# A hybrid decoder layer on one core: one weight split moved, exps and squares exchanged, squares summed four at a time, and a tenth buffer for expert weights

## The reference

```
u = RMSNorm(x);  proj = u @ w_in           # z, xBC, dt, q, k, v, indexer q/k/weights, two gates
A = (RMSNorm(SSD(conv(xBC), dt) * silu(z)) * ssm_norm) @ w_ssm_out   # 32 heads, width 2048
B = DSA attention (indexer picks 64 keys a query, 16 heads) @ w_att_out
x += (sigmoid(gate_ssm)*A + sigmoid(gate_att)*B) @ w_mix_out
x += CrossAttention(RMSNorm(x), RMSNorm(mem))
x += HierarchicalMoE(RMSNorm(x))           # 32 experts of 1024 -> 512 -> 1024, top 2 of 8 in one group
out = RMSNorm(x)
```

## Time and profile before

| What | us |
|---|---|
| Median of 3 runs | 1004.75 |
| Profiled execution, its time | 1004.63 |
| Its span | 1002.9 |
| PE busy | 916.0 |
| DVE busy | 448.9 |
| ACT busy | 308.4 |
| POOL busy | 107.2 |

### The profile page before, as it was taken

The page is one execution under the profiler, slowest core; times in us unless marked ns, Lnnn a source line. Parts: engine busy times, 40 slices in busy tenths (PEclk is TensorE's granted clock), DMA queues, the critical chain, the costliest instruction groups (busy, mean ns, idle before and its releaser), DMA issues.

```text
span 1002.9 us, 13810 instructions
## 1 busy us (share of the span) xinstructions
PE 916.0 (91%) x5693; PEld 634.6 (63%) x5693; DVE 448.9 (45%) x826; ACT 308.4 (31%) x503; POOL 107.2 (11%) x115
## 2 busy tenths in 40 slices
PE   3899889998999999989898999999999898898886
PEld 3799888898889999879675343434343343433432
DVE  5478997676786765365536121212121121211212
ACT  4355445667558443344323000000000000000002
POOL 1000006964662000000000000000000000000000
PEclk9899999999999999999999999999999999999999
DMA  9445354344326667755258999999999999999994
GB/s 217 151 129 179 121 160 143 111 127 127 126 86 178 200 180 283 252 168 210 84 210 323 420 421 421 422 421 421 421 422 421 422 421 422 421 421 421 421 417 172
DMA packets 111896, 278.01 MB, mean 277 GB/s; under 512 B 14866, under 2 KB 78402, under 8 KB 87770
## 3 DMA queue, kind: packets, MB, share of 16 engines
q1 hardware_dynamic: 111690, 276.61, 73.2%
q10 hardware_dynamic: 144, 0.52, 0.1%
HBM read 276.06 MB, written 1.05 MB: 276 GB/s over the span
## 4 chain that ended last, share of the span: by engine, by line
PE 58%; DMA 12%; DVE 11%; SPq 6%; issue 5%; POOL 3%; ACT 3%; DVEq 0%; POOLq 0%; ACTq 0%
PE bank L1876 14%; PE bank L1480 9%; PE bank L1481 9%; PE bank L1482 9%; DMA moe<-in_w_e_up_dram 8%; PE bank L1907 7%; SPq L385 6%; DVE lo_w L915 3%; DMA moe<-in_w_e_gate_dram 3%; POOL work L570 2%; PE bank L1843 2%; PE bank L1893 2%; ACT hi_w L596 1%; DMA moe<-in_w_e_down_dram 1%; DVE work L1072 1%
## 5 line engine op out<-in xcount | busy, mean ns | idle before, releaser
L1876 PE MATMUL bank<-moe,xg 128*64 128x512 f32 x1024 | 228.5, 595 | 19.1 <-DMA moe<-in_w_e_up_dram 9.0
L1480 PE MATMUL bank<-u_hi,hi_w 128*128 128x256 f32 x632 | 184.8, 292 | 11.3 <-DVE lo_w L915 10.4
L1482 PE MATMUL bank<-u_hi,lo_w 128*128 128x256 f32 x632 | 181.1, 286 | 0.0
L915 DVE TENSOR_TENSOR lo_w<-raw_w,hi_w 128x2048 fp32r<-128x2048 f32 x68 | 155.4, 2290 | 56.1 <-ACT hi_w L596 55.8
L1876 PEld LDWEIGHTS bank<-moe,xg 128*64 128x64 f32 x1024 | 74.7, 137 | 156.0 <-issue 153.4
L1481 PE MATMUL bank<-u_lo,hi_w 128*128 128x256 f32 x568 | 163.2, 287 | 0.0
L596 ACT ACTIVATE hi_w<-raw_w 128x2048 fp32r<-128x2048 f32 x68 | 128.5, 1892 | 31.1 <-PE bank L1482 29.2
L1480 PEld LDWEIGHTS bank<-u_hi,hi_w 128*128 128x128 f32 x632 | 123.7, 196 | 15.1 <-issue 10.1
L1482 PEld LDWEIGHTS bank<-u_hi,lo_w 128*128 128x128 f32 x632 | 123.7, 196 | 0.0
L1907 PE MATMUL bank<-moe,moe_buf 128*64 128x512 f32 x480 | 107.0, 596 | 6.1 <-DVE xg L1406 4.7
L1481 PEld LDWEIGHTS bank<-u_lo,hi_w 128*128 128x128 f32 x568 | 111.5, 196 | 0.0
(11 more groups left out here) (310 smaller groups left out, 1373.4 us busy)
## 6 DMA issues: line engine op xcount, KB each, us to landing
moe<-in_w_e_gate_dram SPq DMA_DIRECT2D x64, 1024.0 KB, 26.2
moe<-in_w_e_up_dram SPq DMA_DIRECT2D x64, 1024.0 KB, 26.1
moe<-in_w_e_down_dram SPq DMA_DIRECT2D x64, 1024.0 KB, 26.4
raw_w<-in_w_in_dram SPq DMA_DIRECT2D x34, 1024.0 KB, 5.6
raw_w<-in_w_ssm_out_dram SPq DMA_DIRECT2D x8, 1024.0 KB, 5.8
raw_w<-in_w_xkv_dram SPq DMA_DIRECT2D x8, 1024.0 KB, 5.9
raw_w<-in_w_att_out_dram SPq DMA_DIRECT2D x4, 1024.0 KB, 5.0
raw_w<-in_w_mix_out_dram SPq DMA_DIRECT2D x4, 1024.0 KB, 5.2
```

The source lines that it names most:

```text
L915: tt(lo_w[:, m % RING, 0:w], raw_w[:, m % RING, 0:w], hi_w[:, m % HI_RING, 0:w].bitcast(F32), ALU.subtract).then_inc(lo_done, 1)
L1480: mm(dst, left[0], right[0], start=first, stop=False)
L1482: return mm(dst, left[1], right[0], start=False, stop=last)
L1876: last = mm(ps[64 * a:64 * a + 64, :], xg[:, k, P * o + CAP * a:P * o + CAP * a + CAP], w[:, k % (KT // 2), :], start=(k == 0), stop=(k == ...
```

## The change

1. DVE makes the low part of unit qi1 ahead of the copies of the parameters.
2. In the SSD loop ACT takes the exps of b+1 right after the gate g_b, ahead of the square and `gated_hi`.
3. Squares have six buffers. Four blocks are summed together: four matmuls of 32 columns of ones, each in its own 32 columns of the array, so that each adds its block into its own 32 rows of the bank. They run after y_6, y_10 and y_14 and after ao1. DVE copies the 128 rows of partial sums, PE adds them with one 128x128 matmul after ao2 (each sum comes 32 times, hence the factor), and DVE makes 1/mean after ao2.
4. `moe_buf` becomes a tenth slot, for group 1 alone. Groups 2 to 9 take the slots and the points in SP's order that groups 1 to 8 had, and group 1 is issued behind the second part of group 9. The later groups keep their slots' turn, so group 10 waits for group 0, group 11 for group 2, and so on.

```diff
+        moe_slot.append([moe_buf[:, 0:2048], moe_buf[:, 2048:4096]])
...
+        def turn_of(g):
+            return g if g == 0 else g - 1
         def ring_place(pair, off):
             g = 6 * pair + off
-            return g % MOE_RING, 16 * (g // MOE_RING + 1)
+            if g == 1:
+                return MOE_RING, 16
+            return turn_of(g) % MOE_RING, 16 * (turn_of(g) // MOE_RING + 1)
...
             first_load(7, 1)
             first_load(8, 0)
             first_load(9, 1)
+            over_ring(1, 0, hi_slot=0)
+            over_ring(1, 1, hi_slot=1)
             sp.wait_ge(rl_ready, 2)
...
-            for g in range(MOE_RING, MOE_GROUPS):
-                sp.wait_ge(group_used, g - MOE_RING + 1)
+            for g in range(MOE_RING + 1, MOE_GROUPS):
+                sp.wait_ge(group_used, 1 if g == MOE_RING + 1 else g - MOE_RING + 1)
...
             def square_y(b):
                 act.wait_ge(yg_ready, b + 1)
-                if b >= 2:
-                    act.wait_ge(ssq_mm, b - 1)
-                nc.scalar.activation(ysq[:, b % 2, :], ...
+                if b >= 6:
+                    act.wait_ge(ssq_mm, (b - 6) // 4 + 1)
+                nc.scalar.activation(ysq[:, b % 6, :], ...
...
+            decays(2)
             for b in range(2, 16):
-                decays(b)
                 evac(f"g{b}", gates[:, b, :])
+                if b + 1 < 16:
+                    decays(b + 1)
                 square_y(b - 2)
...
             dve.wait_ge(prm_in, 16 * N_PRM)
+            split_lo_through(UN["qi1"])
             dve.wait_ge(prm_tr, 1)
...
-                    dve.wait_ge(ssq_mm, 16)
-                    link(ts_(rs_bc, bank[2][:, 0:SEQ], 1.0 / D_INNER, EPS, ALU.mult, ALU.add))
+                    dve.wait_ge(ssq_mm, 4)
+                    nc.vector.tensor_copy(rs_bc, bank[2][:, 0:SEQ]).then_inc(ssq_rows, 1)
+                if b == 2:
+                    dve.wait_ge(ssq_mm, 5)
+                    link(ts_(rs_bc, bank[2][:, SEQ:2 * SEQ], 1.0 / (32 * D_INNER), EPS, ALU.mult, ALU.add))
...
-            def sum_squares(b):
-                pe.wait_ge(sq_ready, b + 1)
-                mm(bank[2][:, 0:SEQ], ones[:, :], ysq[:, b % 2, :], start=(b == 0), stop=(b == 15))\
-                    .then_inc(ssq_mm, 1)
+            def sum_squares(j):
+                pe.wait_ge(sq_ready, 4 * j + 4)
+                for a in range(4):
+                    last = mm(bank[2][32 * a:32 * a + 32, 0:SEQ], ones[:, 0:32], ysq[:, (4 * j + a) % 6, :],
+                              start=(j == 0), stop=(j == 3), tile_position=(0, 32 * a))
+                last.then_inc(ssq_mm, 1)
...
-                if b >= 3:
-                    sum_squares(b - 3)
-            sum_squares(13)
+                if b in (6, 10, 14):
+                    sum_squares((b - 6) // 4)
...
-                if b < 2:
-                    sum_squares(14 + b)
+                if b == 1:
+                    sum_squares(3)
+                if b == 2:
+                    pe.wait_ge(ssq_rows, 1)
+                    mm(bank[2][:, SEQ:2 * SEQ], ones[:, :], rs_bc, start=True, stop=True).then_inc(ssq_mm, 1)
```

More of the change, by code:

```diff
@@ L206, in hybrid_block @@
         landed = [sem(f"landed{s}") for s in range(RING)]
-        moe_landed = [[sem(f"moe_landed{s}_{a}") for a in range(2)] for s in range(MOE_RING)]
+        moe_landed = [[sem(f"moe_landed{s}_{a}") for a in range(2)] for s in range(MOE_RING + 1)]
         hi_done = sem("hi_done")
@@ L249, in hybrid_block @@
             sem(n) for n in ("r_ready", "seg_ready", "dec_ready", "m_ready", "y_ready", "y_used"))
-        yg_ready, sq_ready, ssq_mm = sem("yg_ready"), sem("sq_ready"), sem("ssq_mm")
+        yg_ready, sq_ready, ssq_mm, ssq_rows = (sem(n) for n in ("yg_ready", "sq_ready", "ssq_mm", "ssq_rows"))
         y_hi_done, y_lo_done = sem("y_hi_done"), sem("y_lo_done")
@@ L273, in hybrid_block @@
         GATE, UP, DOWN = 0, 2, 4
+        def turn_of(g):
+            return g if g == 0 else g - 1
         def ring_place(pair, off):
             g = 6 * pair + off
-            return g % MOE_RING, 16 * (g // MOE_RING + 1)
+            if g == 1:
+                return MOE_RING, 16
+            return turn_of(g) % MOE_RING, 16 * (turn_of(g) // MOE_RING + 1)
         def loop_place(j, o, off):
-            g = LOOPED + 6 * o + off
+            g = turn_of(LOOPED) + 6 * o + off
             s = g % MOE_RING
-            past = len(range(s, LOOPED, MOE_RING))
-            each = [m for m in range(12) if (LOOPED + m) % MOE_RING == s]
+            past = len(range(s, turn_of(LOOPED), MOE_RING))
+            each = [m for m in range(12) if (turn_of(LOOPED) + m) % MOE_RING == s]
             return s, 16 * (past + each.index(6 * o + off) + 1) + 16 * len(each) * j
@@ L439, in _ @@
                     sp.wait_ge(mix_ready, 8)
-                    first_load(1, 0)
-                    first_load(1, 1)
+                    first_load(2, 0)
+                    first_load(2, 1)
                 if name == "xo00":
-                    first_load(2, 0)
+                    first_load(3, 0)
             def over_ring(g, a, raw_slot=None, hi_slot=None):
@@ L448, in over_ring @@
                 first_load(g, a)
-            over_ring(2, 1, raw_slot=3)
+            over_ring(3, 1, raw_slot=3)
             sp.wait_ge(xo_ready, 2 * X_HEADS)
[L452 to L461, removed]
+            first_load(4, 0)
+            first_load(4, 1)
+            over_ring(5, 0, raw_slot=4)
+            over_ring(5, 1, hi_slot=2)
+            over_ring(6, 0, raw_slot=0)
+            over_ring(6, 1, raw_slot=1)
+            over_ring(7, 0, raw_slot=2)
+            first_load(7, 1)
+            first_load(8, 0)
+            first_load(9, 1)
+            over_ring(1, 0, hi_slot=0)
+            over_ring(1, 1, hi_slot=1)
             sp.wait_ge(rl_ready, 2)
-            first_load(8, 0)
+            first_load(9, 0)
             sp.wait_ge(residual_in, 1)
             sp.wait_ge(xn_lo_done, NT)
-            first_load(7, 1)
-            for g in range(MOE_RING, MOE_GROUPS):
-                sp.wait_ge(group_used, g - MOE_RING + 1)
+            first_load(8, 1)
+            for g in range(MOE_RING + 1, MOE_GROUPS):
+                sp.wait_ge(group_used, 1 if g == MOE_RING + 1 else g - MOE_RING + 1)
                 for a in range(2):
-                    load_part(g % MOE_RING, a, 2 * (g // 6) + a, *load_of(g % 6), by_columns=g >= MOE_GROUPS - 2)
+                    load_part(turn_of(g) % MOE_RING, a, 2 * (g // 6) + a, *load_of(g % 6), by_columns=g >= MOE_GROUPS - 2)
             sp.wait_ge(route_ready, 1)
@@ L757, in square_y @@
                 act.wait_ge(yg_ready, b + 1)
-                if b >= 2:
-                    act.wait_ge(ssq_mm, b - 1)
-                nc.scalar.activation(ysq[:, b % 2, :], ysT[:, b, :], ACT.Square).then_inc(sq_ready, 1)
+                if b >= 6:
+                    act.wait_ge(ssq_mm, (b - 6) // 4 + 1)
+                nc.scalar.activation(ysq[:, b % 6, :], ysT[:, b, :], ACT.Square).then_inc(sq_ready, 1)
             def gated_hi(b):
```

6 lines of the change are left out of this document (3 added, 3 removed).

## The result

| What | us |
|---|---|
| Changed kernel, median of 5 runs | 998.83 (997.61 to 999.40) |
| Kernel before, median of the runs beside them | 1004.86 (1003.68 to 1008.23) |
| Ratio | 0.9938, 95% interval 0.992 to 0.9957 |
| Profiled execution, its time and span | 999.25, 997.5 (before 1004.63, 1002.9) |

The change gives 6.0 us where 10.0 were forecast, and the time lies 0.3 above the upper end of the range. The direction was right.

The account below looks back on a forecast made before the run. Expert weight loading by DMA was taken to set the MoE's pace, with PE and its feeding engines setting its start. Start 6.6, SSD loop 1.1 and tenth slot 2.3 sum to 10.0 off 1004.6: 994.7 us, range 990.5 to 998.5.

Parts of the forecast that it names:

- A: Kernel start: making qi1's low part earlier removes a 4.24 us PE stall and 2.34 us of half clock; 6.6 us.
- B: SSD loop: fewer sums of squares gain 1.6 us, less 0.4 for the matmul after ao2; 1.1 us.
- Behind it waits are relative to one another, up to the MoE.: After the convolution loop's start, the 6.6 us gained at the start carries on to the MoE.
- The sum: Whole kernel: 6.6 + 1.1 + 2.3 = 10.0 us off 1004.6, giving 994.7 us.
- C: MoE start: the tenth slot cuts DMA idle time from 4.9 us to a new gap of 2.6; 2.3 us.
- The gap ahead of group 11: MoE loads: group 11 waits for group 2's slot, leaving DMA idle 2.6 us.
- Later groups come in time: MoE loads after group 11: no further gaps, as PE needs 4.5 us a group and DMA 4.98.
- first rival: Start gives less: the clock falls anyway or DVE or ACT holds the convolution loop; 4.2 or lower, 997 us; chance 0.12.

Follow-up runs that it names:

- A alone: Kernel before with only the low part of qi1 moved ahead of the parameter copies; 998.16 us, ratio 0.9937.
- A and B: As a run: the changed kernel with nine slots, so without the tenth slot; 999.09 us, ratio 0.9944.
- B alone: Changed kernel with the qi1 move and the tenth slot undone, leaving only the SSD edits; 1005.08 us, ratio 1.0009.
- C alone: Kernel before with only the tenth slot and its order of loads; 1003.51 us, ratio 0.9991.
- e3_fill2_after: Changed kernel plus unused matmuls ahead of `vx`, ahead of the first expert and in two waits of the first expert pair; 995.38 us, ratio 0.9911.
- e4_changed: The changed kernel itself, without fill, measured again beside its filled version; 996.44 us, ratio 0.9931.

## Why the prediction was wrong, step by step

**A** (6.6): right. Column 1 is 288.60 before and 282.08 with A alone, 6.5 us. Other executions with the stall have 288.49, 288.07 and 287.86, so 5.8 to 6.5. DVE had its second to spare.

**B** (1.1): right in its sum, and partly by errors that cancel. 282.04 against 280.85 and 282.08 against 280.95, so 1.1 to 1.2. A group makes a step 0.57 longer (4.68 from y_10 to y_11 against 4.11 from y_7 to y_8; I took 0.65), and the exchange in ACT gave nothing. But I had y_5 without a wait, and it waited 0.29 for POOL. So beyond the 6.93 us that y_0 to y_3 already came earlier, y_9 came 0.84 earlier and y_13 1.16, where I had 1.2 and 1.5. ACT took up g_15 1.4 earlier (I had 1.6), and what stands behind it cost 0.3 of that (I had 0.4). A and B together make column 1 7.76 us shorter, where I had 7.7.

**"Behind it waits are relative to one another, up to the MoE."** This is the step that failed. It is true of the waits and not of the clock. I read the clock in the kernel before as a property of its places: half clock behind the stall at 44 us, full clock behind the 2.36 and the 1.99. In the changed kernel's profiled execution the last two fell to half clock. That costs 1.5 us in column 2 (203.18 against 201.7) and 0.4 in column 3, where the stretch stands behind the router logits, and 1.7 in column 4 for the first expert (444.22 against 442.55, B alone). The sum had nothing for it. On which side of the range's end a median then falls is partly luck: the same program measured 998.83 first and 996.44 later, which is inside.

**C** (2.3): hidden in that execution, and too large at full clock. Column 4 became 0.9 longer (443.42 against 442.55). At half clock in the first expert it is 444.22 without the slot (B alone), so that stretch costs 1.7 and the slot gave 0.8; in C alone, with slot and stretch, it is 444.22 as well, and the slot gave nothing. At full clock four executions with the slot have 441.03, 441.33, 441.47 and 442.32, and seven without 442.24 to 442.55: beside the 442.46 of A and B, worth 0.1 to 1.4 us. The gap ahead of group 11, 2.6 in the forecast, is 2.3 in `e3_fill2_after` (windows of 548 to 551 with 205, 25, 172 and 303 GB/s where 421 is full) and 2.8 in the changed kernel's profiled execution, so it was about right. "Later groups come in time" was wrong, by the gap ahead of group 13: 0.4 in `e3_fill2_after` (352 and 303 GB/s at 560 and 561), 1.4 in `e4_changed` (197, 262, 311 and 344 GB/s from 560 to 563). The rest of the lead shrinks later on: in `e4_changed`, where the slot gave 0.1, the parts still land 0.9 us earlier than in the filled kernel without the slot, counted from the first expert matmul, up to the tenth from the end, and 0.1 to 0.2 from the next one on. Why was not tried.

**The sum** for the profiled execution: 7.76 (A, B) - 1.48 (`vx`) - 0.36 (router) - 0.87 (first expert and slot) + 0.31 (it reached the first indexer product earlier) = 5.36, the difference at the last down matmuls. With nothing at half clock the change is worth about 9 us: 995.38 beside 1004.41, and 995.12 beside 1003.93. The forecast of 10.0 was 1 too high there, which is C. The other 1 to 3 us in the unfilled kernel are the clock. My first rival had "the clock falls all the same", but only at the place where it had fallen before.

## What to carry to other kernels

Where PE waits two microseconds or so and does a critical step next, take the full clock behind it as one of two cases, even if a trace shows it, and put the price (here 1.5 to 1.8 us each) in the range; look at several executions, and compare pieces between fixed points, before blaming an edit. Where such a wait can't be removed, unused matmuls into a bank that is free, or a zero block into one that isn't, hold the clock up at no cost that shows here. A further buffer gave back one transfer's idle time here and exposed the next waits of the consumer: walk its order of releases until the loads are again ahead for good.

## What the runs showed of the hardware that was not expected

- The granted clock fell to 0.50 behind idle times of 2.37 and 2.00 us, behind two of 0.96 and 0.83 us with four small transposes between them, and among or behind 32 matmuls of 36 columns, in some executions and not in others. In the two profiled executions of the changed kernel the idle times of 2.37 and 2.00 were the same to 0.01 us.
- Sixteen matmul records of 64 by 512 took 5.35 us with such a stretch in them, and 3.65 without.
- A group of four matmuls of 32 columns of ones by 256 float32, side by side in the array, made a step 0.57 us longer, against 0.44 for one full-width sum. Whether the 0.13 between them is the price of the change of shape can't be told from these runs.
